# Two-block decoder layer on one core: forget gate's chain placed behind the first convolution tiles, first query and key tiles between the two halves of the attention values

## The reference, cut to what matters

```python
def token_mixer(h, w_in, conv_w, conv_b, b_forget, w_conv_out, w_att_out, w_out):
    proj = h @ w_in
    cb, cc, cu, q, k, v, f_logit, g_conv, g_att = split_cols_2(proj)
    y_conv = short_conv(cb, cc, cu, conv_w, conv_b) @ w_conv_out
    o = forgetting_attention(q, k, v, f_logit, b_forget)      # 16 heads of 64
    y_att = o.reshape(B, S, D_ATT) @ w_att_out
    m = sigmoid(g_conv) * y_conv + sigmoid(g_att) * y_att
    return m @ w_out

def forgetting_attention(q, k, v, f_logit, b_forget):
    log_f = log_sigmoid(f_logit + b_forget)
    cum = cumsum(log_f, axis=1)                # one running sum per head
    s = q k^T / 8 + (cum[query] - cum[key])    # causal, by blocks of 128 queries
    return softmax(s) @ v
```

## Time and profile before

| | |
|---|---|
| median of 3 runs | 2816.7 us (2813.88 to 2818.45) |
| profiled execution, its time | 2817.84 us |
| its span in the trace | 2816.2 us |
| TensorE busy | 2660.4 us, 94% |
| VectorE, ScalarE, GpSimd busy | 2014.0, 1292.6, 646.0 us |
| DMA | 609.08 MB, mean 216 GB/s |
| mean granted TensorE clock | 0.975 |

### The profile page before, as it was taken

One profiled execution on the slowest core, in us unless ns is written; L12 is line 12 of the kernel. 1 busy time (PEld: TensorE's weight loads), 2 busy tenths in 40 slices (PEclk: granted clock), 3 DMA queues, 4 the chain that ended last, 5 costly groups with the idle time before them and its releaser, 6 DMA issues. The chain is left out here.

```text
span 2816.2 us, 40392 instructions
## 1 busy us (share of the span) xinstructions
PE 2660.4 (94%) x14563; PEld 1353.1 (48%) x14563; DVE 2014.0 (72%) x3246; ACT 1292.6 (46%) x1379; POOL 646.0 (23%) x479
## 2 busy tenths in 40 slices
PE   6988999999999999999999889999999799999994
PEld 3464544444455554444444444455544455555552
DVE  4545778886688886888888854366543688888885
ACT  5432323323444444333333433344532488888884
POOL 0000000000001013888888300000000322332221
PEclk9988999999999999999999999999999799999997
DMA  5201334433375757999999622211214499999994
GB/s 194 105 31 45 113 113 157 149 143 149 142 224 179 223 180 265 346 364 366 364 364 368 260 105 105 87 63 61 75 60 150 175 387 397 398 400 400 394 400 152
DMA packets 129055, 609.08 MB, mean 216 GB/s; under 512 B 17328, under 2 KB 33712, under 8 KB 79296
## 3 DMA queue, kind: packets, MB, share of 16 engines
q1 hardware_dynamic: 57312, 411.62, 38.4%
q0 software_dynamic: 45024, 149.00, 15.1%
q10 hardware_dynamic: 26624, 47.19, 4.9%
HBM read 539.59 MB, written 68.16 MB: 216 GB/s over the span
## 5 line engine op out<-in xcount | busy, mean ns | idle before, releaser
L695 PE MATMUL ps<-a_hi,w_hi 128*128 128x512 bf16 (+2 forms) x1760 | 649.2, 371 | 11.8 <-ACT arena L1497 7.5
L696 PE MATMUL ps<-a_lo,w_hi 128*128 128x512 bf16 (+2 forms) x1760 | 649.0, 371 | 0.0
L697 PE MATMUL ps<-a_hi,w_lo 128*128 128x512 bf16 (+2 forms) x1760 | 648.6, 371 | 0.0
L695 PE MATMUL ps<-w_hi,arena 128*128 128x512 bf16 (+1 forms) x1600 | 610.0, 381 | 23.4 <-ACT arena L1609 14.6
L697 PE MATMUL ps<-w_hi,arena 128*128 128x512 bf16 (+1 forms) x1600 | 609.3, 381 | 0.0
L696 PE MATMUL ps<-w_lo,arena 128*128 128x512 bf16 (+1 forms) x1600 | 609.2, 381 | 0.0
L1917 DVE TENSOR_TENSOR w_lo<-w_st,w_hi 128x2048 bf16<-128x2048 f32 x127 | 290.9, 2290 | 177.1 <-ACT w_hi L1403 177.1
L1403 ACT ACTIVATE w_hi<-w_st 128x2048 bf16<-128x2048 f32 x127 | 242.3, 1908 | 318.3 <-PE ps L697 316.7
L1409 ACT ACTIVATE xn<-ps 128x512 f32<-128x512 f32 x128 | 76.4, 597 | 428.6 <-PE ps L697 428.6
L695 PEld LDWEIGHTS ps<-a_hi,w_hi 128*128 128x128 bf16 x1760 | 173.0, 98 | 196.3 <-ACT arena L1497 7.6
L697 PEld LDWEIGHTS ps<-a_hi,w_lo 128*128 128x128 bf16 x1760 | 172.8, 98 | 195.9 <-issue 3.5
(11 more groups left out here) (391 smaller groups left out, 3749.5 us busy)
## 6 DMA issues: line engine op xcount, KB each, us to landing
w_st<-in_w_all SPq DMA_DIRECT2D x260, 1024.0 KB, 6.7
arena<-in_w_all SPq DMA_DIRECT2D x64, 1024.0 KB, 9.3
act_dram<-xn POOLq DMA_DIRECT2D x64, 512.0 KB, 2.9
xn<-in_w_all SPq DMA_DIRECT2D x32, 1024.0 KB, 9.2
arena<-act_dram ACTq DMA_DIRECT2D x64, 384.0 KB, 5.3
gate_dram<-arena POOLq DMA_DIRECT2D x7, 3072.0 KB, 19.3
arena<-gate_dram ACTq DMA_DIRECT2D x64, 336.0 KB, 7.1
a_hi<-in_w_all SPq DMA_DIRECT2D x16, 1024.0 KB, 9.3
```

Source lines behind the costliest of these rows:

```text
L695: pe.matmul(dst, l_hi, r_hi, start=start, stop=False)
L696: pe.matmul(dst, l_hi, r_lo, start=False, stop=False)
L697: return pe.matmul(dst, l_lo, r_hi, start=False, stop=stop)
```

## The change

It moves work on three engines. Nothing is computed otherwise, and the number of operations is the same.

- ScalarE: Abs, Exp and Ln become `forget_logs()`, called after the third convolution tile has been copied out (j = 0).
- VectorE: the seven operations become `forget_sums()`, called in the convolution loop behind j = 1. The bias addition stays where it was.
- TensorE: the first query and key tiles (banks 6 and 7) come between the two halves of the values; the second half of the values goes to banks 2 to 5 in place of 4 to 7, since 6 and 7 are taken. The wait for the second half's copies stands at unit 2, the first to use bank 5.
- ScalarE and VectorE copy and split the first queries and keys in that order too, and the `ahead` calls follow.
- Two temporary rows (`n_cum`, `c_rest`) get other addresses, since the convolution's own temporaries are now alive at the same time.

```diff
-        n_cum = view(15360, T)
-        c_rest = view(16384, 2, T)
+        c_rest = view(12288, 2, T)
+        n_cum = view(13312, T)
...
             token_tiles(C_V2, 0, a_hi, a_lo)
             pe.wait_ge(ft_out, F_CONV + 2 * N_CONV)
-            token_tiles(C_V2 + 2, 4, a_hi, a_lo)
+            pe.wait_ge(f_cum, 1)
+            for half in range(2):
+                feature_tile(F_QC + half, CHUNK_QK(0), half, a_hi, a_lo, bank=6 + half)
+            pe.wait_ge(tok_out, TB * (G_V2 - 2 + 1))
+            token_tiles(C_V2 + 2, 2, a_hi, a_lo)
...
-            pe.wait_ge(tok_out, TB * (G_V2 - 2 + 2))
-            pe.wait_ge(f_cum, 1)
-            for half in range(2):
-                feature_tile(F_QC + half, CHUNK_QK(0), half, a_hi, a_lo, bank=6 + half)
...
                         pe.wait_ge(qk_out, 2 * j + 2)
+                    if u == 2:
+                        pe.wait_ge(tok_out, TB * (G_V2 - 2 + 2))
...
                 if j:
                     conv_hi(j - 1)
+                else:
+                    forget_logs()
             conv_hi(KT - 1)
...
+            ahead(C_V2)
+            act.wait_ge(tok_half, G_V2 + 1)
+            ahead(C_V2 + 1)
+            values_out(0)
+            ahead(C_V2 + 2)
             act.wait_ge(f_cum, 1)
             copy_queries(0)
             copy_keys(0)
+            act.wait_ge(tok_half, G_V2 + 2)
+            ahead(C_V2 + 3)
+            values_out(1)
...
                 if j:
                     conv_low(j - 1)
+                if j == 1:
+                    forget_sums()
...
-            for g in range(2):
-                ahead(C_V2 + 2 * g)
-                ahead(C_V2 + 2 * g + 1)
+            for n in range(3):
+                ahead(C_V2 + n)
...
             low_queries(0)
             low_keys(0)
+            ahead(C_V2 + 3)
```

More of the change, by code:

```diff
@@ L1477, in _, with forget_logs @@
                     transposed(3, blocks=[TURNED_AFTER[use, tb]])
[L1479 to L1484, removed]
+            def forget_logs():
+                act.wait_ge(f_xs, 1)
+                act.activation(f_e[0:AH, :], f_x[0:AH, :], ACT.Abs)
+                act.drain()
+                act.activation(f_e[0:AH, :], f_e[0:AH, :], ACT.Exp, scale=-1.0)
+                act.drain()
+                act.activation(f_e[0:AH, :], f_e[0:AH, :], ACT.Ln, bias=ones[0:AH, 0:1]).then_inc(f_ln, 1)
             def conv_hi(j):
@@ L1499, in _ @@
                     conv_hi(j - 1)
+                else:
+                    forget_logs()
             conv_hi(KT - 1)
-            for g in range(2):
-                ahead(C_V2 + 2 * g)
-                act.wait_ge(tok_half, G_V2 + g + 1)
-                ahead(C_V2 + 2 * g + 1)
-                for tb in range(TB):
-                    act.wait_ge(tok_done, TB * (G_V2 + g) + tb + 1)
-                    act.activation(v_s[:, tb, g * 512:(g + 1) * 512], ps[:, 4 * g + tb, :], ACT.Copy).then_inc(tok_out, 1)
             def copy_queries(j):
@@ L1529, in conv_gate, with values_out @@
                 act.activation(sg_s[:, j % 2, :], ps[:, 6, :], ACT.Sigmoid).then_inc(sg_done, 1)
+            def values_out(g):
+                for tb in range(TB):
+                    act.wait_ge(tok_done, TB * (G_V2 + g) + tb + 1)
+                    act.activation(v_s[:, tb, g * 512:(g + 1) * 512], ps[:, 2 * g + tb, :], ACT.Copy).then_inc(tok_out, 1)
+            ahead(C_V2)
[3 more added lines that the diff above has]
+            ahead(C_V2 + 2)
             act.wait_ge(f_cum, 1)
@@ L2078, in _, with forget_sums @@
             dve.tensor_scalar(f_x[0:AH, :], ps[0:AH, 2, :], col("b_forget")[0:AH, :], None, ALU.add).then_inc(f_xs, 1)
[L2079 to L2093, removed]
+            def forget_sums():
+                dve.wait_ge(f_ln, 1)
+                dve.scalar_tensor_tensor(f_x[0:AH, :], f_x[0:AH, :], 0.0, f_e[0:AH, :], ALU.min, ALU.subtract)
+                dve.drain()
+                dve.tensor_tensor_scan(n_cum[0:AH, :], f_one[0:AH, :], f_x[0:AH, :], 0.0, ALU.mult, ALU.subtract)
+                dve.drain()
+                parts = [cum_b[32 * a:32 * a + AH, :] for a in range(3)]
+                dve.tensor_copy(parts[0], n_cum[0:AH, :])
+                dve.drain()
+                dve.tensor_tensor(c_rest[0:AH, 0, :], n_cum[0:AH, :], parts[0], ALU.subtract)
+                dve.drain()
+                dve.tensor_copy(c_rest[0:AH, 1, 0:T // 2].bitcast(BF16), c_rest[0:AH, 0, :])
+                dve.tensor_copy(parts[1], c_rest[0:AH, 0, :])
+                dve.drain()
+                dve.tensor_tensor(parts[2], c_rest[0:AH, 0, :], c_rest[0:AH, 1, 0:T // 2].bitcast(BF16), ALU.subtract).then_inc(f_cum, 1)
+                dve.drain()
             def conv_low(j):
```

## The result

The changed kernel takes 2803.54 us in the median of 5 executions (2796.36 to 2805.82), the kernel before 2817.85: a ratio of 0.9945, with a 95% interval of 0.9929 to 0.9961. In a second session it took 2799.89 us (2795.45 to 2801.90) against 2817.67, a ratio of 0.9938 (0.9926 to 0.9951). So the gain is 14.3 us in the one and 17.8 in the other, where 18.0 was forecast. The time lies in the range and the direction is right. The first session's gain is short by 4 us, which the medians alone would not establish: the two intervals allow gains of 11 to 20 and of 14 to 21 us. The traces show where such a difference comes from, and most of what follows is about that.

The account below looks back on a forecast made before the run. TensorE, busy 94% of the span, was taken as the bound. Terms 7.62 + 2.41 + 0.69 + 5.48 + 2.10 - 0.3 = 18.0 us gave 2799.8 or 2798.7, predicted as 2799.0 us, range 2795 to 2807.

Parts of the forecast that it names:

- The first wait goes whole: At convolution tile 4, TensorE's wait for a weight split goes: 7.62 us, plus 2.41 us for the slow stretch behind it.
- What is late next costs nothing: Work queued behind the moved forget gate chain on ScalarE and VectorE still comes in time; cost nothing.
- Queries and keys between the halves: Waits ahead of the query tile (0.69 us) and first scores (5.48) go; unit 0 at full clock gives 2.10.
- The new entry: At the attention's start the first exponential comes 1.1 us later and TensorE may wait at unit 4: -0.3 us, 0 to -1.2.
- What comes behind follows TensorE: After the attention's entry everything shifts by the same amount; the expert weight loads also start earlier by it.
- router and experts 18 us earlier: Sign expected in the profile after: the router and expert stages start 18 us earlier.
- the slow stretches may differ: Reservation in the range: half-clock stretches may vary between runs; 0.6 us was allowed downward.
- the second rival: The wait ahead of the scores stays or moves to the query tile: up to 7.6 us remain, 2807.4 us, chance 0.07.
- The rule weighed in the prediction: The number of slow matmuls behind a wait is not fixed: 1.3 to 3.0 us for each of the two long waits.
- neither the first nor the second wait stayed: Of these, the first wait's rival: something other than the split is late at convolution tile 4; 2809.9 us, chance 0.06.
- the gain was not given back by the experts' stage: Rival: the experts' loads set their stage and begin at a time not tied to the mixer; 2817 us, chance 0.05.
- the lateness at the entry did not recur: Rival, slower: each of 7 head pairs pays for late queries; 4 us per pair gives 2827.5 us, chance 0.03.

Follow-up runs that it names:

- chain_only: The kernel before with only the forget gate's chain moved behind the first convolution tiles, old order of values, queries and keys; 2806.60 us, ratio 0.9963.
- order_only: The changed kernel with the forget gate's chain back at its old place, so only queries and keys stand between the values' halves; 2807.03 us, ratio 0.9961 against before.
- before_split_late_look: The kernel before with the split of chunk C_AO + 2 put behind the attention loop on ScalarE and VectorE, run once for a profile; 2808.48 us.
- changed_again: The changed kernel, unaltered, run again for a second profile and more executions; 2799.89 us.

## Why the prediction was right, and where it was not

**The first wait goes whole.** Right. The split of C_CONV + 2 starts 0.67 us after the bias addition, the cast at once after the last turned block, and TensorE runs on. Wait and slow stretch were put at 7.62 + 2.41 = 10.0 us; chain_only measured 10.1 by itself. The trace names ScalarE's copy as the releaser, but that of tile 0 was over some 3 us before TensorE started, and the split of the chunk 0.2 us before; this reading made the part safe to predict.

**What is late next costs nothing.** Right, with one date off. Abs came at 1647.2 (1648.52 less 1.35) for a forecast 1647. The sums came at 1661.0 for a forecast 1658, and ended at 1665.8: the second convolution step, behind which they stand, starts with the split of C_CONV + 5, whose cast ScalarE does behind Ln and tile 3's copy (VectorE waits 1.37 us for it, until 1655.5). I had put the end of that cast about right (1654.6, measured 1654.1) and not carried it on to VectorE. It cost nothing, since the first query tile is a hundred us later.

**Queries and keys between the halves.** Right. 0.69 + 5.48 + 2.10 = 8.3 us was the sum, order_only measured 8.2.

**The new entry.** -0.3 us was taken, within 0 to -1.2. Unit 4's scores started 1816.34 - 1803.63 = 12.71 us after unit 0's with no wait. VectorE's low parts of the second queries ended 1815.14 + 1.39 = 1816.53, and the tile that needs them started at 1816.68:

```profile
1815.14 1.39 DVE L2143 SCALAR_TENSOR_TENSOR arena<-ps,arena 64x512 bf16<-64x512 f32 x2 [1.62 <-ACT arena L1512]
```

That is 0.34 us behind the scores, where it was 0.22 before. So the slack of 2.0 us was used up, and exceeded by about 0.1. Two small waits stand in the next pair: 0.2 us, which is new, and 0.6, which was 0.5 before.

**The sum.** 18.0 us forecast, 18.1 and 18.0 measured in the stretch of the change, in two profiles. The kernel before took 206.7 us there in its one profile and 206.5 in that of before_split_late_look, so the measured value is good to some 0.2 us.

**What comes behind follows TensorE.** This is the step that failed, in the sentence that let everything after the attention's entry shift by the same amount. The rest of the program, from the first mixed tile on, did, to within a microsecond: 725.5 us before, 725.7 and 724.8 after. The 240 us between did not. There the same code took 242.4 us in the kernel before and 246.8, or 240.7, in two profiles of the changed one, by how long TensorE fell to half clock behind waits of 0.5 to 3.2 us. So the sign "router and experts 18 us earlier" did not come as written: the first mixed tile came 12.3 us earlier in the one profile (2090.7 to 2078.4) and 21.7 in the other (2069.0), to which the varying start of 1639.6 to 1643.0 us adds its part.

I had read the waits and the clock only in the 220 us around the change, and allowed for the spread of the runs of before, 2.8 us below and 1.8 above the median, taken from three executions. In 15 executions of a later session that kernel spread by 5.5 us, and in 11 of another by 9. The forecast's own "the slow stretches may differ" was the right reservation, with 0.6 us as its size; it measured up to 6.1 (246.8 - 240.7). That the first session's median lies in the range is luck in part: by these terms the range ended at 2802.5, and 2803.5 is inside only since its end had been moved to 2807 for the second rival, which did not come.

The rule weighed in the prediction came true in another place than where I had put it. The traces of this case show, behind one and the same wait of 3.17 us, no half clock at all, 3.4 us of it (the kernel before) or 6.8 (the first profile after). The Trainium skill (TensorE: Matmul & The Clock Gate, What's actually happening) says that the number of slow matmuls differs from run to run of one kernel, and by that rule the trace agrees. I had used it for the two waits that the change removes, where it moves the sum by less than 2 us to either side (the 16.4 to 19.7 us given there leave out the entry's -0.3; with it they are 16.1 to 19.4), and not for the waits that stay.

The rivals: neither the first nor the second wait stayed, the gain was not given back by the experts' stage, and the lateness at the entry did not recur (a pair takes 31.36 us from one gate sigmoid to the next in both kernels).

## What to carry to other kernels

A split, cast or copy that is wanted much later does not belong in front of one that another engine waits for now: reordering alone (the forget gate's chain, the first queries and keys, the splits in the attention loop, a gate tile between the turned groups) took 31.5 us off this kernel, 2817.7 to 2786.2, without taking out one operation. Cut a trace at lines that both kernels have and compare the stretches: that gave the effect of the change to about 0.2 us, where medians of five of the changed kernel differed by 3.65 us between two sessions. And in a TensorE-bound kernel read the granted clock behind every wait in the whole trace, and not only the long ones: a single wait of 3.17 us was a draw for up to 2.9 us more, and groups of waits of 0.5 to 1 us for up to 3.2.

## What the runs showed of the hardware

The fall to half clock behind a wait is not fixed. In one program at one wait of 3.17 us it was 0 us or 6.8 us long in two executions, and the time of the last pair of heads and of the output stage went with it (205.3 + 35.4 against 208.2 + 38.6 us). In the output stretch it followed shorter waits, in two parts of 3.4 us each: one behind waits of 0.54 and 0.47 us of the last units, and one behind waits of 0.98, 0.81 and 0.81 us in the turning of the output. Three profiles have both (38.6 us), five have neither (35.4 us). The last wait ahead of each part, in the first profile after:

```profile
2050.48 1.39 PE L1121 MATMUL ps<-arena 128*128 128x64 f32 x8 [0.47 <-DVE xn L2182]
2064.40 1.72 PE L758 MATMUL ps<-ident,xn 128*128 128x128 f32 x8 [0.81 <-DVE arena L1707]
```

In changed_again the same two groups take 1.08 and 1.26 us. Behind the two long waits that the change removes it came in every profile that had them. What decides between the cases was not tried: no run here varies the moment at which a wait falls by itself.

One execution out of some 80 took 7859.70 us, with a granted clock of 1.00 in the records. Its cause is open.
